# A modulation matrix's first term on ScalarE, a third accumulator, and column sums ahead of the sixth product

## The reference, cut to what matters

```python
h = rmsnorm(x, norm_ffn[L])
x = x + (silu(h @ w_gate[L]) * (h @ w_up[L])) @ w_down[L]      # D_FF = 2816
```

```python
c_act = silu(c)
mods = c_act @ ada_w[i] + ada_b[i]      # 6144 numbers: shifts, scales, gates
```

## Time and profile before

| what | value |
|---|---|
| median of 3 runs | 2073.83 us (2070.13 to 2075.09) |
| the profiled execution's own time | 2073.47 us |
| its span, first to last instruction | 2071.7 us |
| mean granted TensorE clock | 0.970 |
| TensorE busy | 1898.6 us (92%) |
| VectorE busy | 863.3 us (42%) |
| ScalarE busy | 332.1 us (16%) |
| GpSimd busy | 87.1 us (4%) |

### The profile page before, as it was taken

The page is one execution under the profiler, slowest core; times in us unless marked ns, Lnnn a source line. Parts: engine busy times, 40 slices in busy tenths (PEclk is TensorE's granted clock), DMA queues, the critical chain, the costliest instruction groups (busy, mean ns, idle before and its releaser), DMA issues.

```text
span 2071.7 us, 21123 instructions
## 1 busy us (share of the span) xinstructions
PE 1898.6 (92%) x8030; PEld 965.4 (47%) x8030; DVE 863.3 (42%) x1560; ACT 332.1 (16%) x783; POOL 87.1 (4%) x129
## 2 busy tenths in 40 slices
PE   8988999999889999899999999998998999889886
PEld 4555555445555654765434343333775333323321
DVE  1466688834767888765111111112325011111113
ACT  2442111024421111222100010000102000000000
POOL 3102000001020000300000000000000000000000
PEclk9999999999999999999999999999999999999999
DMA  9215767562157677555999999999355999999995
GB/s 309 83 57 163 256 251 279 212 227 62 57 193 288 230 264 264 189 183 191 374 414 428 426 428 428 427 428 407 113 192 214 384 430 428 427 429 427 428 426 232
DMA packets 149241, 603.12 MB, mean 291 GB/s; under 512 B 16584, under 2 KB 60536, under 8 KB 121232
## 3 DMA queue, kind: packets, MB, share of 16 engines
q1 hardware_dynamic: 144064, 591.43, 72.6%
q0 software_dynamic: 4880, 10.22, 1.8%
q10 hardware_dynamic: 192, 0.05, 0.0%
HBM read 597.67 MB, written 1.10 MB: 289 GB/s over the span
## 4 chain that ended last, share of the span: by engine, by line
PE 62%; DMA 24%; DVE 7%; DVEq 2%; issue 2%; ACT 1%; ACTq 1%; SPq 1%
PE ps L2487 14%; DMA ring<-in_e_w_gate 13%; PE ps L907 10%; DMA ring<-in_e_w_up 8%; PE ps L635 7%; PE ps L990 6%; PE ps L2319 4%; PE ps L2505 4%; PE ps L2251 3%; PE ps L2332 3%; PE ps L731 2%; PE ps L2431 2%; PE ps L2416 1%; DMA ring<-in_e_w_down 1%; DMA ring<-in_w_up 1%
## 5 line engine op out<-in xcount | busy, mean ns | idle before, releaser
L2487 PE MATMUL ps<-ring,hT 128*64 128x512 f32 (+1 forms) x1056 | 240.4, 607 | 33.6 <-DMA ring<-in_e_w_up 17.2
L2505 PE MATMUL ps<-ring,qkT 128*64 128x512 f32 (+1 forms) x1024 | 226.6, 594 | 9.9 <-ACT qkT L2707 7.9
L2487 PE MATMUL ps<-ring,late 128*32 128x512 f32 (+1 forms) x928 | 211.1, 609 | 24.0 <-DMA ring<-in_e_w_up 12.7
L635 PE MATMUL ps<-ring,hT 128*128 128x512 f32 (+1 forms) x384 | 169.3, 592 | 3.0 <-DMA ring<-in_w_in 2.2
L2487 PEld LDWEIGHTS ps<-ring,hT 128*64 128x64 f32 (+1 forms) x1056 | 77.3, 126 | 193.1 <-issue 193.1
L2976 DVE TENSOR_TENSOR qkT<-ps,qkT 128x512 f32<-128x512 f32 (+1 forms) x64 | 44.2, 690 | 255.6 <-PE ps L2505 255.6
L2999 DVE TENSOR_TENSOR qkT<-ps,qkT 128x512 f32<-128x512 f32 (+1 forms) x32 | 22.1, 690 | 297.8 <-PE ps L2487 297.8
L2487 PEld LDWEIGHTS ps<-ring,late 128*32 128x32 f32 (+1 forms) x928 | 68.6, 125 | 161.9 <-issue 161.9
L2505 PEld LDWEIGHTS ps<-ring,qkT 128*64 128x64 f32 (+1 forms) x1024 | 70.9, 123 | 146.2 <-issue 146.2
L1612 DVE SCALAR_TENSOR_TENSOR qkT<-ring,cc,qkT 128x512 f32<-128x512 f32 x168 | 125.9, 749 | 8.5
L635 PEld LDWEIGHTS ps<-ring,hT 128*128 128x128 f32 x384 | 72.3, 195 | 80.0 <-issue 70.3
(11 more groups left out here) (433 smaller groups left out, 2238.8 us busy)
## 6 DMA issues: line engine op xcount, KB each, us to landing
ring<-in_e_w_down SPq DMA_DIRECT2D x64, 2048.0 KB, 17.0
ring<-in_e_w_up SPq DMA_DIRECT2D x64, 2048.0 KB, 17.3
ring<-in_e_w_gate SPq DMA_DIRECT2D x60, 2048.0 KB, 17.5
ring<-in_ada_w SPq DMA_DIRECT2D x24, 2048.0 KB, 14.2
ring<-in_w_gate SPq DMA_DIRECT2D x16, 1408.0 KB, 8.7
ring<-in_w_up SPq DMA_DIRECT2D x16, 1408.0 KB, 9.3
ring<-in_w_down SPq DMA_DIRECT2D x22, 1024.0 KB, 5.1
ring<-in_w_in SPq DMA_DIRECT2D x8, 2048.0 KB, 11.6
```

The costliest lines, as they stand in the source:

```text
L635: last = mm(m.ps[:, 4 + i, 0:chunk_width(n)], m.hT[:, j, i * P:(i + 1) * P], w[:, j, :], start=(j == 0), stop=(j == KC - 1))
L2487: last = mm(dst, xg[:, j, at + x * n_tok:at + x * n_tok + place], w(x, j), start=(j == 0), stop=(j == KC - 1))
L2505: lasts[x] = mm(dst, m.hidT[:, j, rows + x * place:rows + (x + 1) * place], half_of(w(x, j), n), start=(j == 0), stop=(j == 3))
```

## The change

- **Terms.** Term (k, 0) goes from VectorE to ScalarE: `ada_begun(k)` makes it as a Copy with the scale c's column 0. It waits for the slice's load (`ada_full`) and, from slice 3 on, for the column sum of slice k - 3. VectorE's term (k, 1) waits for the load and for ScalarE. The terms of a step still count (k, 0).
- **Accumulators.** Three (N_ACC) take turns for two.
- **Where ScalarE does it.** ADA_BEGUN[n]: at the head of step n, ahead of `kept(n-1, "P5")`, or in the down part ahead of the copy `turned`; ADA_LATER[k]: after the silus of the step, ahead of `kept(k, "P6")`. With the new ADA_TERMS that gives the head of steps 0, 1, 2, 7 (slices 0, 1, 2, 8) and of 9, 11, 14 (slices 9, 10, 11), and the later place in steps 2 to 6 (slices 3 to 7).
- **silu21** on ScalarE goes behind `kept(k, "P6")` in odd steps.
- **Terms by step.** ADA_TERMS changes: slices now end in steps 1, 1, 2, 3, 4, 5, 6, 7, 9, 11, 14, 16. So slices 0 and 1 are summed in step 2, slice 8 in step 10; loads of slices 3 and 10 move (3 to n = 2, 10 to n = 10).
- **Column sums** go ahead of P6 in an up step; their results go to banks 6 and 7 in turn.
- **SP's queue**: up_load(1) goes ahead of ada(1).

The diff, cut to its core:

```diff
@@ -102,18 +102,46 @@
         SUMMED += [("c21", _k - 1)] + ([("hid21", _k - 1)] if _k % 2 == 0 else [])
 SUMMED += [("down", _c) for _c in range(1, N_DC)]
 
+N_ADA = 12
+N_ACC = 3
+ADA_SLOTS = (0, 1, 5)
+
+
+N_STEPS = N_FU + N_DC
+ADA_TERMS = [7] + [9] * 6 + [7] + [2, 4, 4] + [3] * 6 + [0] * (N_DC - 9)
+ADA_FIRST = [sum(ADA_TERMS[:n]) for n in range(N_STEPS + 1)]
+assert ADA_FIRST[-1] == N_ADA * KC
+
+
+def ada_step(k):
+
+    return next(n for n in range(N_STEPS) if ADA_FIRST[n + 1] >= KC * (k + 1))
+
+
+ADA_SUMMED = [[k for k in range(N_ADA) if ada_step(k) + 1 == n] for n in range(N_STEPS)]
+ADA_ROWS = [[k for k in range(N_ADA) if ada_step(k) + 2 == n] for n in range(N_STEPS + 1)]
+ADA_LOADS = [[k for k in range(3, N_ADA) if max(ada_step(k - 2), 1) + 1 == n] for n in range(N_STEPS)]
+ADA_BEGUN = [[k for k in range(N_ADA) if ADA_FIRST[n] <= KC * k < ADA_FIRST[n] + 4 and KC * k < ADA_FIRST[n + 1]] for n in range(N_STEPS)]
+ADA_LATER = [[k for k in range(N_ADA) if ADA_FIRST[n] + 4 <= KC * k < ADA_FIRST[n + 1]] for n in range(N_FU)]
+
 TAKEN = []
 for _k in range(N_FU):
+    TAKEN += [("ada", _n) for _n in ADA_BEGUN[_k]]
     if _k > 0:
         TAKEN.append(("P5", _k - 1))
     TAKEN.append(("P1", _k))
     if _k % 2 == 0:
         TAKEN.append(("silu11", _k))
     else:
-        TAKEN += [("silu22", _k - 1), ("silu12", _k - 1), ("silu21", _k - 1)]
+        TAKEN += [("silu22", _k - 1), ("silu12", _k - 1)]
+    TAKEN += [("ada", _n) for _n in ADA_LATER[_k]]
     TAKEN.append(("P6", _k))
+    if _k % 2 == 1:
+        TAKEN.append(("silu21", _k - 1))
 TAKEN.append(("P5", N_FU - 1))
-TAKEN += [("turned", _c) for _c in range(N_DC)] + [("last", 0)]
+for _c in range(N_DC):
+    TAKEN += [("ada", _n) for _n in ADA_BEGUN[N_FU + _c]] + [("turned", _c)]
+TAKEN.append(("last", 0))
 FF_ORDER = {"product": PRODUCTS, "summed": SUMMED, "taken": TAKEN}
 
 
@@ -131,25 +159,6 @@
 
 OUT_BANK = (6, 3, 0, 1, 0)
 OUT_PARTS = ((4, 0, 2), (2, 0, 2), (0, 0, 1), (6, 0, 2), (0, 1, 2))
-
-N_ADA = 12
-ADA_SLOTS = (0, 1, 5)
-
-
-N_STEPS = N_FU + N_DC
-ADA_TERMS = [6] + [9] * (N_FU - 1) + [3] * 9 + [0] * (N_DC - 9)
-ADA_FIRST = [sum(ADA_TERMS[:n]) for n in range(N_STEPS + 1)]
-assert ADA_FIRST[-1] == N_ADA * KC
-
-
-def ada_step(k):
-
-    return next(n for n in range(N_STEPS) if ADA_FIRST[n + 1] >= KC * (k + 1))
-
-
-ADA_SUMMED = [[k for k in range(N_ADA) if ada_step(k) + 1 == n] for n in range(N_STEPS)]
-ADA_ROWS = [[k for k in range(N_ADA) if ada_step(k) + 2 == n] for n in range(N_STEPS + 1)]
-ADA_LOADS = [[k for k in range(3, N_ADA) if max(ada_step(k - 2), 1) + 1 == n] for n in range(N_STEPS)]
 
 N_UNITS = len(UNITS)
 
@@ -298,7 +307,7 @@
     m.act_sum = m.O[:].rearrange("p i c -> p (i c)").rearrange("p (s j t) -> p s j t", s=4, j=KC // 2)
     m.hid = m.z[:].rearrange("p i c -> p (i c)")[:, 0:TILES * D_FF].rearrange("p (i f) -> p i f", i=TILES)
     m.hidT_a = [at.rearrange("p (k t) -> p k t", k=8) for at in (m.late[:, 0:8 * P], m.hT[:, 0:4, :].rearrange("p j t -> p (j t)"))]
-    m.ada_acc = q[:, 7168:8192].rearrange("p (b n) -> p b n", b=2)
+    m.ada_acc = q[:, 7168:8704].rearrange("p (b n) -> p b n", b=N_ACC)
     m.ada_b = q[:, 5632:7168].rearrange("p (k n) -> p k n", k=N_ADA)
     m.mrow = q[:, 8704:8704 + 2 * P].rearrange("p (b n) -> p b n", b=2)
     at = QK_AT
@@ -463,8 +472,8 @@
 
         up_load(0)
         ada(0)
+        up_load(1)
         ada(1)
-        up_load(1)
         ada(2)
         for n in range(2, N_STEPS):
             if n < N_FU:
@@ -952,13 +961,13 @@
                 if n < N_FU:
                     if L > 0 or k >= 2:
                         ready("ada_row", k - 1)
-                    dst = m.ps[:, 6, k % 2 * P:(k % 2 + 1) * P]
+                    dst = m.ps[:, 6 + k % 2, 0:P]
                 else:
                     taken("turned", min(n - N_FU + 1, N_DC - 1))
                     ready("ada_row", k)
                     dst = m.ps[:, 7, 0:P]
                 for g in range(4):
-                    last = mm(dst[32 * g:32 * (g + 1), :], m.ones[:, 0:32], m.ada_acc[:, k % 2, g * P:(g + 1) * P], start=True, stop=True)
+                    last = mm(dst[32 * g:32 * (g + 1), :], m.ones[:, 0:32], m.ada_acc[:, k % N_ACC, g * P:(g + 1) * P], start=True, stop=True)
                 last.then_inc(s["ada_ps"], 1)
 
         def hid_transposes(c):
@@ -966,7 +975,7 @@
             summed("hid21", 2 * hid_unit(c) + 1)
             if c > 0:
                 taken("turned", c - 1)
-            rows = [k for n in range(N_FU, N_FU + c - 1) for k in ADA_SUMMED[n]]
+            rows = [k for n in range(N_FU + c - 1) for k in ADA_SUMMED[n] if n >= N_FU or k % 2 == 1]
             if rows:
                 ready("ada_row", rows[-1] + 1)
             for i in range(TILES):
@@ -1009,8 +1018,8 @@
             up_product(k - 1, "P3")
             up_product(k, "P2")
             up_product(k - 1, "P4")
+            ada_sums(k)
             up_product(k, "P6")
-            ada_sums(k)
             up_product(k, "P7")
             up_product(k, "P5")
         hid_transposes(0)
@@ -1242,7 +1251,17 @@
                 summed({(0, 0): "c11", (1, 1): "c22", (1, 0): "c21"}[i, h], k)
             a(out, src, ACT.Silu).then_inc(s["taken"], 1)
 
+        def ada_begun(k):
+
+            act.wait_ge(s[f"ada_full{k % 3}"], nth(L, f"ada_full{k % 3}", 16 * (k // 3 + 1)))
+            if L > 0 or k >= N_ACC:
+                act.wait_ge(s["ada_ps"], nth(L, "ada_ps", k - N_ACC + 1))
+            w = m.slot[ADA_SLOTS[k % 3]].rearrange("p (j n) -> p j n", j=KC)[:, 0, :]
+            a(m.ada_acc[:, k % N_ACC, :], w, ACT.Copy, scale=m.cc[:, 0:1]).then_inc(s["taken"], 1)
+
         for k in range(N_FU):
+            for n in ADA_BEGUN[k]:
+                ada_begun(n)
             if k > 0:
                 kept(k - 1, "P5")
             kept(k, "P1")
@@ -1251,12 +1270,17 @@
             else:
                 gated(k - 1, 1, 1)
                 gated(k - 1, 0, 1)
+            for n in ADA_LATER[k]:
+                ada_begun(n)
+            kept(k, "P6")
+            if k % 2 == 1:
                 gated(k - 1, 1, 0)
-            kept(k, "P6")
             for n in ADA_ROWS[k]:
                 ada_store(n)
         kept(N_FU - 1, "P5")
         for c in range(N_DC):
+            for n in ADA_BEGUN[N_FU + c]:
+                ada_begun(n)
             product("turned", c)
             if c == 1:
                 product("P4", N_FU - 1)
@@ -1601,15 +1625,13 @@
         def ada_term(k, j):
 
             if j == 0:
+                return
+            if j == 1:
                 dve.wait_ge(s[f"ada_full{k % 3}"], nth(L, f"ada_full{k % 3}", 16 * (k // 3 + 1)))
-                if L > 0 or k >= 2:
-                    dve.wait_ge(s["ada_ps"], nth(L, "ada_ps", k - 1))
+                taken("ada", k)
             w = m.slot[ADA_SLOTS[k % 3]].rearrange("p (j n) -> p j n", j=KC)[:, j, :]
-            acc = m.ada_acc[:, k % 2, :]
-            if j == 0:
-                ts(acc, w, m.cc[:, 0:1], None, ALU.mult)
-            else:
-                last = stt(acc, w, m.cc[:, j:j + 1], acc, ALU.mult, ALU.add)
+            acc = m.ada_acc[:, k % N_ACC, :]
+            last = stt(acc, w, m.cc[:, j:j + 1], acc, ALU.mult, ALU.add)
             if j == KC - 1:
                 last.then_inc(s["ada_red"], 1)
             if j == KC - 1 and k >= N_ADA - 3:
@@ -1624,7 +1646,7 @@
             dve.wait_ge(s["ada_ps"], nth(L, "ada_ps", k + 1))
             if L > 0 or k >= 2:
                 dve.wait_ge(s[f"ada_out{k % 2}"], nth(L, f"ada_out{k % 2}", 16 * (k // 2)))
-            src = m.ps[:, 6, k % 2 * P:(k % 2 + 1) * P] if ada_step(k) + 1 < N_FU else m.ps[:, 7, 0:P]
+            src = m.ps[:, 6 + k % 2, 0:P] if ada_step(k) + 1 < N_FU else m.ps[:, 7, 0:P]
             tt(m.mrow[:, k % 2, :], src, m.ada_b[:, k, :], ALU.add).then_inc(s["ada_row"], 1)
 
         def ada_terms(lo, hi):
```

## The result

The changed kernel takes 2056.06 us (median of 4 runs, 2053.08 to 2057.34) against 2072.23 us before (4 runs, one more than stood behind the 2073.83 above; 2070.13 to 2075.09) on the same chip: ratio 0.9919, 95% interval 0.9901 to 0.9937, or 16.2 us less. The forecast was 7.1 us less, 2066.7 us. The profiled execution took 2057.34 us (span 2055.5), so span against span is 16.2 us less too. 2056.06 lies on the lower edge of the range given (2056 to 2075): the gain is more than twice the forecast.

The account below looks back on a forecast made before the run. TensorE was taken to bound the feed-forwards, so only its waits could be won. Removed waits less added ones gave -3.1 us in layer 0 and -4.0 in layer 1, together -7.1: 2066.7 us, range 2056 to 2075.

Parts of the forecast that it names:

- the removed waits: TensorE's up-phase waits for w_up (3.1 us, layer 0) and ScalarE before P5(3) (4.6 us, both layers) go, with slow clock behind.
- place 2: ScalarE's wait for ada(8) ahead of kept(6, P5) delays P3(6): 2.4 us in layer 0, 1.9 in layer 1.
- The prize: Time won in the feed-forwards by ending TensorE's waits: 15.8 us in layer 0, 9.2 in layer 1.
- place 1: ScalarE's wait for ada(1) ahead of kept(0, P5) delays P3(0): 2.8 us in layer 0, 0.2 in layer 1.
- slow clock behind place 1: Granted clock falls after the new gap before P3(0) in layer 0: 3.0 us (0 to 3.0).
- slow clock behind place 2: Granted clock falls after the new gaps before P3(6): 2.3 us in layer 0, 1.6 in layer 1.
- place 3: ScalarE's wait for ada(10) ahead of the copy of turned(3), third down chunk: 2.2 us in layer 0, about 1.5 in layer 1.
- Theory C: Set at the experiments' start: the clock falls elsewhere by luck, and that is the whole gain; no chance given.

Follow-up runs that it names:

- x4_begun_behind: Changed kernel with ScalarE's first term of a step moved behind the copies of P5(k-1) and P1(k): 2053.51 us, ratio 0.9914 to the kernel before.
- a0_after: The changed kernel itself, unaltered, timed again on another chip: 2057.78 us, ratio 0.9934 to the kernel before.
- x5_silu_first: Changed kernel with silu21 again ahead of the copy of P6 in odd steps: 2058.08 us, ratio 0.9947 to the kernel before.
- x7_sums_behind: Changed kernel with the column sum behind P6 again, three accumulators kept: 2059.16 us, ratio 0.9941 to the kernel before.
- z1_longer_gap: Changed kernel with ScalarE writing term (8,0) three times more before its signal: 2067.38 us, ratio 0.9978 to the kernel before.
- x1_swap_only: Kernel before with one edit, up_load(1) ahead of ada(1) on SP's queue: 2067.75 us, ratio 0.9986 to the kernel before.
- y2_third_acc: x1_swap_only plus a third accumulator, with the sums in banks 6 and 7 by turns: 2049.57 us, ratio 0.9908 to the kernel before.
- x2_no_swap: Changed kernel with SP's old order, ada(1) ahead of up_load(1): 2064.80 us, ratio 0.9960 to the kernel before.
- z3_third_alone: Kernel before with only three accumulators (sums in banks 6 and 7 by turns), no swap: 2054.53 us, ratio 0.9926 to the kernel before.
- y4: x1_swap_only plus the changed kernel's shares of terms by step (ADA_TERMS): 2065.19 us, ratio 0.9971 to the kernel before.
- y1: x1_swap_only plus the column sum ahead of P6, two accumulators: 2055.11 us, ratio 0.9941 to the kernel before.
- x3_term_vector: Changed kernel with the first term of each matrix slice back on VectorE: 2051.89 us, ratio 0.9907 to the kernel before.

## Why the prediction was wrong

The direction was right, and so were the removed waits and place 2; the sum was 9 us short. What the change adds was priced at 17.9 us and took 7.5. The prize was 0.6 us larger than priced, and 2.3 us came back between the feed-forwards, which the prediction put at nothing ("the gain carries to the end"). Term by term, measured from the table:

| term (layer 0; layer 1) | priced | measured | from |
|---|---|---|---|
| prize of the removed waits | -15.8; -9.2 | -16.1; -9.5 | x4_begun_behind's up less before's |
| place 1, ada(1) before P3(0) | +2.8; +0.2 | 0; 0 | timeline: P3(0) on time |
| slow clock behind place 1 | +3.0 | 0 | no gap |
| place 2, ada(8) before P3(6) | +2.4; +1.9 | +2.7; +2.1 | after's up less x4_begun_behind's |
| slow clock behind place 2 | +2.3; +1.6 | 0; 0 | products of 2.60 us |
| place 3, third down chunk | +2.2; +1.5 | +1.1; +1.6 | after's down less before's |
| sum | -7.1 | -18.1 | |
| between the feed-forwards | 0 | +2.3 | after's 181.94 less 179.66 |

**The step that failed first is place 1's landing,** worth 5.8 us with the slow clock priced behind it. The prediction took 209.5 us for ada(1) (bounds 207.5 and 212), since the fourth place "needs the same bytes" as the fourth load of before. It landed at 205.9, outside the bounds; ScalarE's wait for it ended in time, P3(0) did not wait, nor did it in the four other traces with this order and the term at this place (a0_after, x5_silu_first, x7_sums_behind, z1_longer_gap). The stretches from 185 to 189, to 193 and to 209 us, of the kernel before and then of the changed one (length, busy times, clock, DMA share, GB/s):

```profile
185.00:189.00 4.00, 3.53 (x9) 1.58 (x9) 3.18 (x6) 1.96 (x3) 4.00 (x7) 1.00 1.06 195
189.00:193.00 4.00, 3.09 (x16) 2.16 (x15) 3.36 (x11) 1.44 (x5) 1.38 (x3) 1.00 0.93 226
193.00:209.00 16.00, 11.71 (x43) 6.74 (x41) 11.16 (x17) 4.09 (x9) 0.00 (x0) 0.98 1.04 347
```

```profile
185.00:189.00 4.00, 3.53 (x9) 1.58 (x9) 3.17 (x8) 1.96 (x3) 4.00 (x7) 1.00 0.99 98
189.00:193.00 4.00, 3.08 (x16) 2.11 (x15) 3.40 (x11) 1.43 (x5) 1.41 (x3) 1.00 0.85 204
193.00:209.00 16.00, 15.09 (x55) 9.25 (x54) 14.22 (x20) 6.16 (x13) 0.00 (x0) 1.00 1.05 389
```

In the kernel before, ada(1) was issued at 178 and flowed among GpSimd's small loads (issued 179 to 190), of which one took 12.8 us to land; now the large loads start at 189.3, when the small ones are nearly through, and run at 389 instead of 347 GB/s. w_up(1) landed at 200.5, not 203 to 204. From 195 to 201 us, in steps of 2 us, x1_swap_only and y2_third_acc, with the same order, move 374 to 406 GB/s; before, x2_no_swap and z3_third_alone, with the old one, 280 to 382. That the small loads' draining is the cause is read from this pairing and was not tried by itself. The Trainium skill ("DMA: Bandwidth & Descriptors", "Issuing engines are not separate DMA queues") says that transfers from all issuers share the same 16 engines and interleave; these rows agree.

The rate is the smaller part, though. By 206 us SP's queue had moved 7.50 MB in the kernel before and 7.68 MB in the changed one, 0.2 MB apart. From 177 us to the landing of the fourth load (209.2, then 205.9) it moved (packets, MB, share of the 16 engines):

```profile
q1 hardware_dynamic: 4946, 8.69, 80.0%
```

```profile
q1 hardware_dynamic: 4437, 7.65, 74.8%
```

The four loads are 7.08 MB (two of 2048 KB, two of 1408 KB). So 1.6 MB of the fifth load, ada(2), had gone through before w_up(1) was complete, and only 0.6 MB of it before ada(1) was: 1.0 MB, or 2.7 us at 389 GB/s, of the 3.3 us between the two landings. The 17 traces sort the same way: 7.6 to 8.1 MB at this landing in the 14 kernels with up_load(1) ahead, 8.4 to 8.7 in the three with the old order. So "the same bytes" was wrong by the bytes of the load behind. Why less of ada(2) ran ahead, though it was issued earlier (193.6 for 197.4 us), no run shows.

**The second is the clock behind new gaps,** worth 3.9 us. The prediction priced it at 2.3 and 1.6 us for gaps of 2.4 and 1.9, by one precedent of 2.16 us against one of 1.5 us without it. That precedent came from the attention stretch ahead of the feed-forward, and there the clock behaves otherwise: the gap of 2.15 to 2.17 us before the matmuls of that row has slow clock behind it in all 17 traces, but inside the up phases the gaps of all traces sort so:

- 1.75 to 1.83 us (P3(6) of layer 1 in after, x2, x5, x7, a0; y4's P5(3) twice): slow clock in none of 7.
- 2.13 to 2.49 us (P3(6) of layer 0; y1's P5(3) twice; w_up in x2 and z3): slow in 4 of 9, each worth 1.7 to 2.1 us. At P3(6) alone it is 2 of 5.
- 3.06 us and more (before, x1, z1): slow in 7 of 7, 1.5 to 3.0 us.

Place 2's two gaps of 2.45 and 1.83 us would by these counts be priced as a chance of about a half on 1.8 us in layer 0 and as nothing in layer 1: near 1 us, not 3.9. That the slow clock stayed away in both profiles of the changed kernel was in part luck. The Trainium skill ("TensorE: Matmul & The Clock Gate", "What's actually happening") says that the activity monitor runs freely and doesn't start with the kernel, so the place of a change varies; the same gap at the same place with and without slow clock, in x7_sums_behind (2.49) and in the first trace (2.45), agrees with that.

**Right.** The prize to 0.6 us; that ScalarE's work itself is hidden and its wait for ada_w is what costs; place 2 to 0.3 us; place 3's mechanism. At the third down chunk both layers of the changed kernel have gaps of 0.52 and 0.83 us, 1.35 together, where 2.2 and 1.5 were priced; that layer 1's total of 1.6 us meets the 1.5 is partly luck, as 0.37 us of it stand elsewhere (the gap ahead of its first down chunk's P6 is 1.30 us for 0.93). In layer 0 the place was too dear because ada(10) was issued at 344.46 and landed 9.9 us later, not 11.2. ScalarE's term lasts 0.72 us, not 0.62, which by 24 terms is 5.5 us more than 24 of VectorE's 0.49, and costs nothing, being off the path: the Trainium skill's rule that multiplies belong on VectorE ("ScalarE: Activation LUTs", "Rules for kernel authors") speaks here through the waits, not through the durations. x3_term_vector, which follows it, is the faster kernel.

**What the gain is made of.** The accumulator alone (z3_third_alone) has the ratio 0.9926 where the whole change has 0.9919 and 0.9934: it ends a stall that is there in both layers, which the swap can't. The sum ahead of P6 does about the same work as the accumulator and halves the stall alone; with both, one of them is spare. The first term on ScalarE costs about 4 to 6 us against leaving it on VectorE. Theory C falls as the cause of the gain: the up phases are 20.9 us shorter, at the removed waits and the slow clock behind them, and where the clock fell elsewhere, between the feed-forwards, it cost time.

**Open.** "Between" grew from 179.66 to about 181.5 us in nearly every faster kernel. The stretch before and after, with the same 716 matmuls:

```profile
424.60:604.30 179.70, 166.15 (x716) 97.57 (x716) 90.27 (x226) 69.25 (x193) 18.53 (x28) 0.97 0.32 101
```

```profile
412.30:594.20 181.90, 168.18 (x716) 97.99 (x716) 90.08 (x226) 69.07 (x193) 18.52 (x28) 0.96 0.30 96
```

TensorE is busy 2.0 us longer at a mean clock of 0.96 for 0.97, so it is mostly clock, not waits. The granted clock is 0.50 for 10.2 us of this stretch in the kernel before and in z1_longer_gap (179.66 and 179.95 us) and for 13.7 us or more in the other fifteen (180.9 to 182.1 us); 3.4 us more at half clock are 1.7 of the 2.3 us. No instruction there was changed, and it doesn't follow the start of the stretch: z1_longer_gap starts it at 419.63, x2_no_swap, with 182.11 us, at 420.24. What decides it, no run settles. What follows layer 1's feed-forward varies more, from 1233.4 to 1242.4 us over the 17 traces, also without a changed instruction; so medians here can differ by some us from what the stretches say.

## What to carry to other kernels

Where an engine waits to reuse an accumulator, one more of them ends the wait, and its worth can be read beforehand: not the whole wait (5.63 us) but TensorE's own stall behind it (4.58), and the slow clock after that. When work goes to an idle engine, price not its duration but what its first instruction waits for and what stands behind it in that engine's order; moving the waiting instruction behind two copies gave back 4.8 us of stretch here. And a load's time to landing is that of its company: take the rate from a stretch in which the same neighbours are in flight, and count the bytes of the load issued behind it, which can go through first. A precedent for the clock should come from the same kind of stretch.

## What the runs showed of the hardware

- Inside the up phases, a gap of TensorE of 2.1 to 2.5 us took the clock to 0.50 in 4 of 9 cases, with the same gap at the same place going either way; none of 1.8 us did (7), all of 3 us and more did (7).
- In the attention stretches (90 to 180 us and their like in layer 1) it fell more readily: behind gaps of 2.15 to 2.20 us in 51 of 51 cases, behind gaps of 1.83 to 1.96 us in 24 of 85 (counted over all traces, by a granted clock under 0.9 in the 2 us behind the gap). So length alone does not decide.
- A load issued later takes its share before the earlier one is complete: of ada(2) (2.1 MB, issued at 197.4 us) 1.6 MB had gone through when the w_up issued at 189.8 landed at 209.2.
- An ACTIVATE of 128x512 with its factor read from a column of SBUF took 0.72 us here, and the next starts 0.63 us after it; the one in the rows of before took 0.62. The Trainium skill ("ScalarE: Activation LUTs", "What ACT_TABLE_LOAD costs") gives a fixed part, a part for each pointer operand and a rate per element from which I work out an estimate of 0.71 us; the trace agrees.
- With 18 small loads of GpSimd (128 KB at most) in flight beside large ones, the 16 DMA engines were as busy as ever (share 1.06, 0.93) at 195 and 226 GB/s; without them 389 GB/s were moved at a share of 1.05.
